# Stick-breaking attention in head pairs: both heads of a turn go through logits, softening, sums and values together

## The reference, cut to what matters

```python
z = jnp.einsum('bhqd,bhkd->bhqk', qi, kf) * scale
mask = key_pos[None, :] < q_pos[:, None]
log_fail = jnp.where(mask, jax.nn.log_sigmoid(-z), 0.0)
after = lax.cumsum(log_fail, axis=3, reverse=True) - log_fail
w = jnp.where(mask, jnp.exp(jax.nn.log_sigmoid(z) + after), 0.0)
return jnp.einsum('bhqk,bhkd->bhqd', w, vf)
```

## Time and profile before

| | us |
|---|---|
| median of 3 runs | 4058.1 (4056.68 to 4061.71) |
| profiled execution, its time | 4059.52 |
| its span | 4057.8 |
| PE busy | 3633.8 (90%) |
| DVE busy | 2603.7 (64%) |
| POOL busy | 1433.5 (35%) |
| ACT busy | 1116.9 (28%) |

### The profile page before, as it was taken

One profiled execution on the slowest core, in us unless ns is written; L12 is line 12 of the kernel. 1 busy time (PEld: TensorE's weight loads), 2 busy tenths in 40 slices (PEclk: granted clock), 3 DMA queues, 4 the chain that ended last, 5 costly groups with the idle time before them and its releaser, 6 DMA issues.

```text
span 4057.8 us, 51253 instructions
## 1 busy us (share of the span) xinstructions
PE 3633.8 (90%) x13950; PEld 2299.6 (57%) x13950; DVE 2603.7 (64%) x5393; ACT 1116.9 (28%) x2531; POOL 1433.5 (35%) x1220
## 2 busy tenths in 40 slices
PE   4999898999866999998979998989998579999987
PEld 2444444777654448873445454457767544588633
DVE  6444214898987777676654451169998777676665
ACT  1333211323287003330023231023224940133100
POOL 0000001445433665566500000014544345656663
PEclk9999999999977999999989998999998789999999
DMA  6221122888855999999942212248877579999997
GB/s 246 102 104 47 66 100 104 306 317 310 301 161 174 405 399 395 341 373 384 389 187 93 93 43 98 79 173 319 315 296 270 162 256 401 405 380 346 384 386 308
DMA packets 278115, 1016.53 MB, mean 251 GB/s; under 512 B 31354, under 2 KB 48250, under 8 KB 266882
## 3 DMA queue, kind: packets, MB, share of 16 engines
q0 software_dynamic: 157696, 570.50, 37.5%
q1 hardware_dynamic: 120194, 443.42, 29.0%
HBM read 988.63 MB, written 25.17 MB: 250 GB/s over the span
## 4 chain that ended last, share of the span: by engine, by line
PE 48%; DVE 22%; DMA 10%; ACT 7%; issue 6%; DVEq 5%; POOL 1%; ACTq 1%; SPq 0%; POOLq 0%
PE ps L604 16%; PE ps L783 8%; PE ps L557 6%; DMA arena<-in_u_dram,idx 5%; DVE mod L1414 4%; PE ps L515 4%; DVE arena L1408 3%; DVE arena L1196 3%; ACT mod L949 2%; ACT mod L945 2%; PE ps L658 2%; DMA hT<-gate_scratch 2%; DMA arena<-in_v_dram,idx 2%; PE ps L492 2%; PE ps L612 2%
## 5 line engine op out<-in xcount | busy, mean ns | idle before, releaser
L1155 POOL DMA_INDIRECT arena<-in_u_dram,idx x512 | 665.5, 1300 | 986.4 <-issue 656.9
L557 PE MATMUL ps<-hT,mod 128*128 128x256 f32 x4096 | 926.9, 379 | 0.0
L604 PE MATMUL ps<-arena 128*128 128x512 f32 x2048 | 888.3, 597 | 33.4 <-DVE arena L1458 29.7
L1155 POOL DMA_INDIRECT arena<-in_v_dram,idx x512 | 650.4, 1270 | 633.9 <-DVE mod L1414 379.7
L557 PEld LDWEIGHTS ps<-hT,mod 128*128 128x128 f32 x4096 | 759.6, 190 | 93.0
L1408 DVE CUSTOM_DVE_ANT_0 arena<-arena 128x1024 f32<-128x1024 f32 x512 | 616.4, 1224 | 248.2 <-DMA arena<-in_u_dram,idx 244.8
L1414 DVE SCALAR_TENSOR_TENSOR mod<-arena,mod 128x1024 f32<-128x1024 f32 x512 | 657.1, 1283 | 139.0 <-DMA arena<-in_v_dram,idx 110.9
L604 PEld LDWEIGHTS ps<-arena 128*128 128x128 f32 x2048 | 391.7, 191 | 527.5 <-issue 527.4
L977 ACT COPY mod<-ps 128x512 f32<-128x512 f32 x512 | 274.6, 590 | 555.9 <-PE ps L547 555.5
L1134 POOL TENSOR_SCALAR_AFFINE_SELECT arena<-arena 128x128 f32<-128x128 f32 x64 | 19.9, 311 | 824.9 <-ACT arena L1055 824.9
L547 PE MATMUL ps<-const,arena 128*128 128x128 f32 x2048 | 269.0, 275 | 16.3 <-ACT mod L977 15.5
(11 more groups left out here) (196 smaller groups left out, 3715.4 us busy)
## 6 DMA issues: line engine op xcount, KB each, us to landing
arena<-in_u_dram SPq DMA_DIRECT2D x256, 512.0 KB
arena<-in_v_dram SPq DMA_DIRECT2D x256, 512.0 KB
arena<-in_ada_w_dram SPq DMA_DIRECT2D x56, 1024.0 KB, 6.0
hT<-gate_scratch POOLq DMA_DIRECT2D x128, 256.0 KB, 10.5
arena<-in_w_qkv_dram SPq DMA_DIRECT2D x48, 512.0 KB, 6.2
arena<-in_w_m_dram SPq DMA_DIRECT2D x16, 1536.0 KB, 6.7
arena<-in_w_q_dram SPq DMA_DIRECT2D x32, 576.0 KB, 6.7
gate_scratch<-hT SPq DMA_DIRECT2D x64, 256.0 KB, 2.1
```

The lines of the kernel that those rows point to most:

```text
L557: last = pe.matmul(ps[:, 6 + tile // 2 % 2, tile % 2 * NT:(tile % 2 + 1) * NT], u_turned[:, tile % 2, k * P:(k + 1) * P], hT[:, k, DT0:SEQ ...
L604: last = pe.matmul(ps[:, 2 * c + n, :], act_t[:, e, c * P:(c + 1) * P], stream[:, slot, n * 512:(n + 1) * 512], start=(half == 0 and e == ...
L1155: pool.indirect_dma_start(out=ring[:, r % RING, :], out_offset=None, in_=table, in_offset=bass.IndirectOffsetOnAxis(ap=idx[:, j % 4, k:k + ...
```

## The change

The four key blocks are now steps p = 0 to 3 and each step carries both heads. PE issues the logits of both heads one behind the other, in banks 2 and 3 for even p and 4 and 5 for odd p, with no wait between them; head 0 uses rows 0 to 63 of the array, head 1 rows 64 to 127. The sums are accumulated onto these same banks, so the second computation of the logits is gone. The two value matmuls of a step also follow each other without a wait, head 0 in columns 0 to 63 of the array, head 1 in 64 to 127. The weights have four buffers, two of them in `h_row`. ACT runs each pass of the softening over both heads before the next pass, and DVE does the same. The key projection of the differential head (group 4) is cut in two halves around the logits of step 2. The differential section, the modulation and everything outside `mix` keep their instructions.

```diff
@@ PE
+                def project_half(g, bank, ks):
+                    for k in ks:
+                        last = pe.matmul(ps[:, bank, :], w_qkv[:, g, k, :], hT[:, k, :], start=(k == 0), stop=(k == KD - 1))
+                    return last
+                def logits(p):
+                    kb = CH - 1 - p
+                    if p == 0:
+                        pe.wait_ge(S["q_ev"], i + 1)
+                        pe.wait_ge(S["k_ev"], i + 1)
+                        pe.wait_ge(S["p_exp"], 8 * i + 1)
+                    elif p == 1:
+                        pe.wait_ge(S["wt_ev"], CH * i + 1)
+                    else:
+                        pe.wait_ge(S["w_exp"], 8 * i + 2 * p - 2)
+                    for h in range(2):
+                        r = slice(HD * h, HD * h + HD)
+                        pe.matmul(ps[:, 2 + 2 * (p % 2) + h, 0:qcols(kb)], sb_k[r, kb * P:(kb + 1) * P],
+                                  sb_q[r, kb * P:SEQ], start=True, stop=True).then_inc(S["z_done"], 1)
+                def sums(p):
+                    kb = CH - 1 - p
+                    for h in range(2):
+                        bank = 2 + 2 * (p % 2) + h
+                        pe.wait_ge(S["L_done"], 8 * i + 2 * p + h + 1)
-                        logits(b, bank, False)
                         last = pe.matmul(ps[:, bank, 0:qcols(kb)], C(NEG_UPPER), L[:, h, kb, 0:qcols(kb)],
...
+                def values(p):
...
+                    pe.wait_ge(S["w_masked"], 8 * i + 2 * p + 2)
+                    for h in range(2):
                         pe.matmul(ps[HD * h:HD * h + HD, 6, kb * P:SEQ], sb_v[:, kb * P + HD * h:kb * P + HD * h + HD],
-                                  w_att[:, b % 2, 0:qcols(kb)], start=(kb == CH - 1), stop=(kb == 0),
+                                  w_att[2 * (p % 2) + h][:, 0:qcols(kb)], start=(kb == CH - 1), stop=(kb == 0),
...
+                logits(0)
+                logits(1)
+                project(i, 3, 0)
+                mod_block(n0 + 2, 2)
+                sums(0)
+                pe.wait_ge(w_in[4], 16 * i + 16)
+                project_half(4, 1, range(0, 4))
+                logits(2)
+                project_half(4, 1, range(4, KD)).then_inc(proj[4], 1)
+                sums(1)
...
+                values(0)
+                logits(3)
...
+                project_v(5, 7, [0])
+                sums(2)
...
+                values(1)
+                project_v(5, 7, [1]).then_inc(S["dv_mm"], 1)
+                sums(3)
+                values(2)
+                values(3)
@@ ACT
+                def soften(p):
+                    n = qcols(CH - 1 - p)
+                    for h in range(2):
+                        act.wait_ge(S["z_done"], 8 * i + 2 * p + h + 1)
+                        if p >= 1:
+                            act.wait_ge(S["L_done"], 8 * i + 2 * p + h - 1)
+                        act.activation(soft[:, h, 0:n], ps[:, 2 + 2 * (p % 2) + h, 0:n], ACT.Abs)
+                    act.drain()
...
+                soften(0)
+                soften(1)
+                act.wait_ge(proj[3], i + 2)
+                act.mul(dq_raw, ps[:, 0, :], SCALE).then_inc(S["dqraw_ev"], 1)
+                mod_evac(n0 + 2, TURN_BLOCKS * t + 2)
+                weigh(0)
+                soften(2)
+                act.wait_ge(proj[4], i + 2)
+                act.copy(dk_raw, ps[:, 1, :]).then_inc(S["dkraw_ev"], 1)
+                weigh(1)
+                soften(3)
+                weigh(2)
+                weigh(3)
@@ DVE
+                for p in range(CH):
+                    for h in range(2):
+                        dve.wait_ge(S["ln_done"], 8 * i + 2 * p + h + 1)
+                        dve.scalar_tensor_tensor(L[:, h, kb, 0:n], ps[:, 2 + 2 * (p % 2) + h, 0:n], 0.0, soft[:, h, 0:n],
                                                  ALU.max, ALU.add)
-                        dve.drain()
+                    dve.drain()
+                    for h in range(2):
                         dve.tensor_tensor(L[:, h, kb, 0:P], L[:, h, kb, 0:P], C(STRICT), ALU.mult).then_inc(S["L_done"], 1)
```

More of the change, by code:

```diff
@@ L167, in build @@
         lam_prod = part(A_W + 4 * HD, 2, HD)
[L168 removed]
+        w_a = part(A_W, 2, SEQ)
+        w_att = [w_a[:, 0, :], w_a[:, 1, :], h_row[:, 0:SEQ], h_row[:, SEQ:2 * SEQ]]
         qkv = part(A_QKV, 8, SEQ)
@@ new lines, in mix @@
+                mod_block(n0 + 2, 2)
[5 more added lines that the diff above has]
+                sums(1)
+                pe.wait_ge(S["dqraw_ev"], i + 1)
+                pe.matmul(ps[:, 0, :], C(ROPE_PERM), dq_raw, start=True, stop=True).then_inc(S["rope_mm"], 1)
+                values(0)
+                logits(3)
@@ L703, in mix @@
+                pe.wait_ge(w_in[5], 16 * i + 16)
+                project_v(5, 7, [0])
+                sums(2)
+                pe.wait_ge(S["dkraw_ev"], i + 1)
+                pe.matmul(ps[:, 1, :], C(ROPE_PERM), dk_raw, start=True, stop=True).then_inc(S["rope_mm"], 1)
+                values(1)
[3 more added lines that the diff above has]
+                values(3)
                 pe.wait_ge(S["dq_ready"], i + 2)
@@ new lines, in soften @@
+                def soften(p):
[7 more added lines that the diff above has]
+                    for h in range(2):
+                        act.activation(soft[:, h, 0:n], soft[:, h, 0:n], ACT.Exp, scale=-1.0)
+                    act.drain()
+                    for h in range(2):
+                        act.activation(soft[:, h, 0:n], soft[:, h, 0:n], ACT.Ln, bias=1.0).then_inc(S["ln_done"], 1)
@@ new lines, in weigh @@
+                def weigh(p):
+                    n = qcols(CH - 1 - p)
+                    for h in range(2):
+                        act.wait_ge(S["b_done"], 8 * i + 2 * p + h + 1)
+                        act.wait_ge(S["pv_done"], 8 * i + 2 * p + h + 1)
+                        act.activation(w_att[2 * (p % 2) + h][:, 0:n], ps[:, 2 + 2 * (p % 2) + h, 0:n],
+                                       ACT.Exp).then_inc(S["w_exp"], 1)
+                soften(0)
+                soften(1)
+                act.wait_ge(proj[3], i + 2)
@@ L1133, in _ @@
                         park()
-                        pool.affine_select(out=w_att[:, u % 2, 0:P], in_=w_att[:, u % 2, 0:P], compare_op=ALU.is_gt,
+                        pool.affine_select(out=w_att[u % 4][:, 0:P], in_=w_att[u % 4][:, 0:P], compare_op=ALU.is_gt,
                                            fill=0.0, base=0, pattern=[[1, P]], channel_multiplier=-1
```

67 lines of the change are left out of this document (16 added, 51 removed).

## The result

The changed kernel takes 3953.5 us (the median of 3953.5, 3957.7 and 3944.5) against 4057.4 for the one before, a ratio of 0.974 (95% interval 0.9727 to 0.9753). A fourth execution, 7230.6 us at a mean granted clock of 0.487, is left out; with it the median is 3955.6. The forecast was 3969 and its range ended at 3957, so the gain was under-estimated: 106.0 us between the profiled executions (4059.52 to 3953.50) where 89.6 were forecast.

A forecast was written before the change was run, and what follows sets the result against it. PE's stream was taken to bound the stick-breaking section: 5.46 + 2.90 + 2.80 + 0.20 - 0.16 = 11.2 us a turn, 89.6 over eight turns, from 4059.5 to 3969.9, forecast as a median of 3969 us, range 3957 to 3991.

The forecast's parts named there:

- What bounds the section: Stick-breaking section: PE's stream sets the time, busy for 48.31 of 48.73 us, with one gap of 0.35.
- Walking the waits: Check of PE's waits in the section's new order: other engines finish in time, tightest slack 0.5 to 1.5 us.
- tight places: Waits before logits of steps 2 and 3: slack 0.5 to 1.5 us and near 0.9 us.
- the last gap: PE's wait before the values of the last block, where POOL's mask comes last: stays at 0.35 us.
- Column halves: Both heads' value matmuls of a step run side by side: 2.8 us less a turn, with no row showing it.
- Row halves: Both heads' logits of a step run side by side, the second head free: 2.90 us less a turn.
- rival 4: PE's clock falls in the section, making the kernel slower than before, up to 4269 us; chance 0.02.
- smaller terms: In the section: head 1's sums following head 0's save 0.2 us a turn; the cut key projection costs 0.16 more.
- three large terms: Per turn: second logits gone 5.46 us, logits paired on row halves 2.90, values paired on column halves 2.80.
- cut projection's own cost of 0.16: Key projection cut in two loses one hidden weight load: 1.05 - 0.895 = 0.16 us more a turn.
- rule on weight loads: Trainium skill: loads overlap running matmuls only when row groups differ; for value pairs it would cost 8.6 us; chance 0.08.

The follow-up runs named there:

- full second logits: Kernel before with only the second logits computed on all 128 rows instead of 64; 4038.7 us against 4054.9.
- full logits: Changed kernel with both logits of a step computed on all 128 rows, so no longer side by side; 3950.6 us.
- joined values: Changed kernel with earlier first differential logits and later value-projection quarters, plus step 0's value pair moved next to step 1's; 3926.1 us, ratio 0.9684.

## Why the prediction was wrong

- **What bounds the section** was right: PE's stream, before and after, with 0.35 us of gap in 35.28. Walking the waits was right too; none of the tight places opened, and the last gap stayed at 0.35 as said. The walk missed one wait of the kernel before, the 0.29 at the modulation block in six of the eight sections, which went away.
- **Column halves**, the open cost, came out as taken: the pair steps at 0.37 and 1.01. **Row halves** as well, 1.06 at 512 columns. **Clock**: 1.00 as before, so rival 4 did not occur. The differential section kept its length.
- **The step that failed is the one on smaller terms.** It gave a change of form between matmuls at most 0.11 us at four places, 0 to 0.44 a section, with 0.2 taken. It is 0.15 to 0.23 us at each change: 0.218 in the kernel before with full second logits, where nothing else changes; 0.227 in the one without them, 0.176 with full logits and 0.20 with the second logits put back (7.43 - 4.27 = 3.16 over 16 changes), each after taking off the streaming; 0.15 with joined values. And 23 changes went. The 0.15 is a single change less, the one into half columns; that it is the smallest fits its shorter weight loads (0.13 us against 0.19 on the full array), but is one case.
- **How the terms look in these units.** Streaming that went: 4.27 for the second logits, 2.13 for each pairing, 8.53. The section lost 13.16 in the first turn of a layer and 13.45 in the others. Less the wait of 0.29, that leaves 4.63 for changes of form, 0.20 each. The three large terms of the prediction, 5.46, 2.90 and 2.80, held 2.63 of this, since a matmul's step before contained its own share of the changes around it: the late load in front and the late start of the next one behind. The smaller terms added 0.04. The share in its neighbours' steps the prediction left there: 4.63 - 2.67 = 1.96 a section, 15.7 us in all. With the wait, six times 0.29 = 1.7, that is 17.4, and so much more than the forecast did the span lose (107.0 - 89.6).
- **Where the row showed it.** The sum behind logits, 0.42 against 0.31, was read as a cost of the first matmul behind a change and taken for head 1's sums alone; the permutation between two logits was not looked at:

```profile
219.87 1.13 PE L650 MATMUL ps<-arena,const 128*128 128x512 f32 x2
220.93 0.48 PE L658 MATMUL ps<-arena 64*128 64x128 f32 x2
```

  It took 1.06 for 512 columns, while eight in a chain took 0.895 each (0.87 without the wait behind them) and 512 columns among their own form 0.86. The prediction read the difference as a hidden weight load of a long chain, where the loads show that what counts is the form of the matmul in front. The cut projection's own cost of 0.16 was too high: its halves take 3.53 each, 7.06 together, 0.09 more than the uncut projection beside it (6.97).

The Trainium skill's page "TensorEngine Tiling (Array Packing)", section "Tiling Modes", says that changing the tiling mode, not just the tile, drains TensorE. The runs agree, in that no weight load goes ahead across a change, and put a number on it, about 0.2 us a change. The prediction left this rule out; with 23 changes at 0.2 in place of what the steps held, an estimate made now from the runs, it would have said 8.53 + 4.6 = 13.1 us a section, some 3953. The rule on weight loads that it weighed instead changes nothing here: the column halves share all rows and still step as one, 1.01 us at 512 columns.

## What to carry to other kernels

Where PE's stream is the bound, write it down as a row of tile forms and count the changes; a small matmul of another form costs its columns and two changes, about half of that in its neighbours' steps. Price a removed instruction by the streams with and without it and not by its own step. When logits are cheap in columns, half-array matmuls pay only in pairs or in groups: one alone costs more than on the full array (0.62 against 0.43 at 256 columns). On the full array, though, these logits sum both heads; whether zeros in the other head's rows, which would make them right, are worth their cost was not tested. Once the stream is short, look at what stands ahead of the next chain's first link; starting that link earlier and moving two fillers behind it gave 32 us here, a third of what the change itself gave, some 18 of it from the turns at an equal clock. And compare versions by stretches with the same granted clock before calling an edit worthless or explaining what is left over.

## What the runs showed of the hardware that was not expected

A change between full-array and half-array matmuls in float32 costs 0.15 to 0.23 us, spread over the steps on both sides: a 512-column matmul took 1.06 between two of another form and 0.86 among its own. The weight load, which stands 0.1 to 0.43 us ahead of a matmul behind one of its own form, starts with the matmul at a change. Half-column pairs overlap as fully as half-row pairs, 1.01 for two against 1.81 when both use the same columns. A half-row pair of 384 columns takes 0.85 and the same two on the full array 1.29. By the same steps the pair should save nothing at 128 columns, where two sums on the full array take 0.44 (186.56 to 187.00) and the pair 0.42; this is an estimate, no run tries it.
